# A one-core layer stack on Trainium2: expert gates spread by bf16 one-hot products, the gate in three bf16 parts

## The chip, the cores and the metric

The kernel runs on one core of one Trainium2 chip. The metric is the device time of one execution in microseconds (us). It is computed from fp32 inputs to an fp32 output.

## The reference, cut to what matters

Two blocks follow each other on 512 tokens of width 1024. The first ends in a product-key retrieval of single-neuron experts (`peer_ffn`): each token picks, for each of 8 heads, 16 of 16,384 experts, so 128 experts a token, each with a softmax gate.

```python
def block(args):
    x_blk, i_blk, g_blk = args
    act = jnp.einsum('td,ted->te', x_blk, u[i_blk]).astype(f32)
    hid = jax.nn.gelu(act, approximate=False) * g_blk
    return jnp.einsum('te,ted->td', hid.astype(v.dtype), v[i_blk])
```

An expert's number is 128 times a row index plus a column index, both from 0 to 127.

## The kernel before, in words

All big products are made from operands split into two fp32r halves: `split_hi` (ScalarE, L281) rounds a weight tile of 128x1024 from `wraw` to `wh`, `split_lo` (L289, VectorE or GpSimd) forms the rest `wl`, and `three` (L300 to L302) issues three matmuls, high by high, low by high, high by low. `wh` and `wl` have four buffers, so ScalarE may write the high half of tile m+4 only when TensorE is done with tile m, and VectorE waits for ScalarE.

The experts are computed in two ways. For 384 of the 512 tokens (`ND`), TensorE computes all 16,384 activations x·u as 128 tiles (`up_pe`, L300 to L302 with 384 columns; eight chunks `kc` of three matmuls a tile), ScalarE applies gelu and SyncE stores the result in DRAM. For these tokens the gates must be spread over a matrix of 128x128 per token that is zero but at the 128 chosen experts. The other 128 tokens gather their rows of u by indirect DMA (`fetch_pool`, L1844), and VectorE takes 128 dot products (L1834, 1.22 us each, one or two in a stage, by the table `DOT`).

The gate matrix of a token is one matmul over the 128 slots: the stationary operand holds, for each slot, the one-hot row of its row index times the slot's gate; the moving operand holds the one-hot row of its column index. Both are fp32, and a gate product (`gate_pe`, L1715) shows as two matmul records and two weight loads. The engines walk through the 128 tiles in the same order, each with a list of stages m:

- Slots are turned onto partitions in stages 27, 37 and 47 (`TURN`): TensorE transposes three matrices (row index, column index, gate) of 128 tokens, and ScalarE copies them to `iT` (L1789).
- In 48 of the 73 stages from 48 to 120 (`GATE`: k for stage 48 + 74k/48) VectorE forms the one-hot tiles of eight tokens, group k: two equality comparisons of 128x1024 (L1822), then the product by the gate for tokens 4 to 7 (L1827). ScalarE multiplies tokens 0 to 3 by the gate, one by one (L1780). The tiles have two buffers; one is called `oh`, the other is part of `under`, and VectorE waits until the products of group k-2 are done.
- Two stages later (`GMUL`) TensorE makes the eight gate products of group k, one after each chunk of three matmuls. The first waits for both equalities and the first of ScalarE's products, the fifth for L1827.
- ScalarE copies the banks of four tokens to `gbuf` (L1761), SyncE stores finished blocks of 64 tokens (L1909).

VectorE's order in a stage is: `split_lo` of tile m+4, the second top-k (up to stage 44), the one-hot tiles, the dot products.

```python
    GATE = {48 + k * 74 // NG: k for k in range(NG)}
    GMUL = {m + 2: k for m, k in GATE.items()}
    for _k in range(SP):
        DOT.setdefault(46 + _k * 81 // SP, []).append(_k)
```

Of the 48 groups, 26 come in a stage whose forerunner has none, and 22 in a stage right behind another group's; of these 22, 13 have two dot products in the stage before and 9 have one.

Of the kernel before, what the change touches and what calls it, by code (L numbers as in the profile page):

```python
# [15 lines left out]
SP = 128  # L16
ND = T - SP
# [57 lines left out]
def build_program(nc, A, out):  # L75
    ctx = ExitStack()

    def sb(name, shape, dt=F32, scope=None):
        return (scope or ctx).enter_context(nc.sbuf_tensor(name, shape, dt))

    def sem(name):
        return ctx.enter_context(nc.semaphore(name))
# [17 lines left out]
    under = sb("under", [128, 2, 8, T])  # L100
# [12 lines left out]
    iota = sb("iota", [128, 128])  # L113
# [43 lines left out]
    gsp = sb("gsp", [128, SP], scope=peer)  # L157
    hid = sb("hid", [128, SP], scope=peer)
    turned = ExitStack()
    iT = sb("iT", [128, 3, ND], scope=turned)  # L160
    oha = sb("oh", [128, 2, 8, 128], scope=turned)
    rest = sb("rest", [128, max(4, 3 * NR + 6 * ND - 3 * ND - 2048)], scope=turned)
    top = ExitStack()
    qb = sb("qb", [128, 2, T], scope=top)
# [56 lines left out]
    fetch = [b.rearrange("p a t -> p (a t)") for b in (tmpb[:, 0:2, :], tmpb[:, 2:4, :], rsb[:, 0:2, :], sqdg[:, :, :])]  # L221


    oh = [[oha[:, w, :, :] for w in range(2)], [under[:, w, :, 0:128] for w in range(2)]]

    vg = [vgt[:, i, :] for i in range(4)]
    va = vat[:, 5:7, :].rearrange("p a t -> p (a t)")
# [65 lines left out]
    freed = {}  # L293
# [1288 lines left out]
    s_itp, s_it = sem("s_itp"), sem("s_it")  # L1582
    s_idx, s_gsp = sem("s_idx"), sem("s_gsp")
    s_gl = sem("s_gl")
    s_gas = [sem(f"s_gs{i}") for i in range(NL)]
    s_oh, s_os = sem("s_oh"), sem("s_os")
    s_gm, s_gb, s_gst = sem("s_gm"), sem("s_gb"), sem("s_gst")
    s_rsum, s_rtp, s_rx = sem("s_rsum"), sem("s_rtp"), sem("s_rx")
    s_f = [sem(f"s_f{i}") for i in range(len(fetch))]
# [25 lines left out]
    def second_dve(dve, tc, part):  # L1615

        k2, n0 = tc % 2, SEC_N * tc
        if part == 0:
            if tc == 3:
                dve.wait_ge(s_it, 1)  # L1620
            if tc == 2:
                dve.wait_ge(s_gsp, 16 * (128 // SP))
                dve.wait_ge(s_idx, 2 + 16 * (128 // SP))
            dve.wait_ge(s_top, top_count(15, tc, 5))
            dve.tensor_copy(tif[:, k2, :, :], ti[:, tc, :, :]).then_inc(s_sec, 1)
# [75 lines left out]
    def gate_bank(q):  # L1701
        return 5 + q % 3

    def gate_pe(pe, i):

        k, j = i // 8, i % 8
        b = gate_bank(i // 4)
        if i % 4 == 0:
            bank_free(pe, b)
        if j < 4:  # L1710
            pe.wait_ge(s_oh, 3 * k + 2)
            pe.wait_ge(s_os, 4 * k + j + 1)
        else:
            pe.wait_ge(s_oh, 3 * k + 3)
        pe.matmul(ps[b][:, (i % 4) * 128:(i % 4 + 1) * 128], oh[k % 2][0][:, j, :], oh[k % 2][1][:, j, :], start=True,  # L1715
                  stop=True).then_inc(s_gm, 1)
        freed[b] = (s_gb, i // 4 + 1)

    def up_pe(pe):
        def each(m, kc):  # L1720
            if m == 0 and kc in (1, 5):
                score_pe(pe, 14 if kc == 1 else 15)
            if m in GMUL:
                gate_pe(pe, 8 * GMUL[m] + kc)

        for m in range(128):
            pe_linear(pe, W_U, [m], B_U, None, lambda g: (s_gl, g + 1), t0=SP, each=each)
            if m in TURN:
                tc = TURN[m]
                b = gate_bank(tc)  # L1730
                pe.wait_ge(s_sec, SEC_N * (tc + 1))
                bank_free(pe, b)
                for w in range(3):
                    mm = pe.transpose(ps[b][:, w * 128:(w + 1) * 128], slot[:, tc % 2, w, :], ident[:, :])
                mm.then_inc(s_itp, 1)
                freed[b] = (s_it, tc)
# [15 lines left out]
    def gate_copy(act, q):  # L1752

        half, at = gate_half(4 * q)
        block = 4 * q // BW
        act.wait_ge(s_gm, 4 * q + 4)
        if q == 0:
            act.wait_ge(s_it, 3)
        if block >= 2:
            act.wait_ge(s_gst, 16 * 16 * (block - 1))  # L1760
        act.activation(gb[:, half, :, at:at + 4], ps[gate_bank(q)][:, :].rearrange("p (t i) -> p i t", t=4),  # L1761
                       ACT.Copy).then_inc(s_gb, 1)

    def up_act(act):
        for m in range(128):
            split_hi(act, W_U + m + 4)
            act.wait_ge(s_wuse, W_U + m + 1)
            if m >= NL:
                act.wait_ge(s_gas[m % NL], 16 * (m // NL))
            act.activation(gl[:, m % NL, :], ps[B_U[m]][:, SP:T], ACT.Gelu).then_inc(s_gl, 1)  # L1770
            if m in GMUL:
                gate_copy(act, 2 * GMUL[m])
                gate_copy(act, 2 * GMUL[m] + 1)
            if m in GATE:
                k = GATE[m]
                act.wait_ge(s_oh, 3 * k + 1)
                for j in range(4):
                    t = 8 * k + j
                    o = oh[k % 2][0][:, j, :]
                    act.activation(o, o, ACT.Copy, scale=iT[:, 2, t:t + 1]).then_inc(s_os, 1)  # L1780
            if m in EXPS:
                tc = EXPS[m]
                g = slot[:, tc % 2, 2, :]
                act.wait_ge(s_sec, SEC_N * tc + 50)
                act.activation(g, g, ACT.Exp).then_inc(s_secx, 1)
            if m in TURN:
                tc = TURN[m]
                act.wait_ge(s_itp, tc)
                act.activation(iT[:, :, tc * 128 - SP:tc * 128 + 128 - SP],  # L1789
                               ps[gate_bank(tc)][:, 0:384].rearrange("p (w t) -> p w t", w=3),  # L1790
                               ACT.Copy).then_inc(s_it, 1)
            if m == ROWTURN:
                for half in range(2):
                    act.wait_ge(s_rtp, half + 1)
                    act.activation(xrow[:, half * 512:(half + 1) * 512], ps[6 + half][:, :],
                                   ACT.Copy).then_inc(s_rx, 1)
            if m >= 126:
                hh_act(act, m - 126)

    def up_dve(dve):  # L1800
        for m in range(128):
            if W_U + m + 4 not in U_POOL:
                split_lo(dve, W_U + m + 4)
            if m >= 126:
                h_lo(dve, m - 126)
            if m == ROWSUM:
                x3 = fetch[0].rearrange("p (c t) -> p c t", t=128)
                for c in (14, 15):
                    dve.wait_ge(*XL["q"][c])
                for s in range(128 // SP):  # L1810
                    dve.tensor_tensor(x3[:, :, SP * s:SP * s + SP], Xh[:, :, 0:SP].bitcast(F32),
                                      Xl[:, :, 0:SP].bitcast(F32), ALU.add).then_inc(s_rsum, 1)
            for tc, part in SEC.get(m, ()):
                second_dve(dve, tc, part)
            if m in GATE:
                k = GATE[m]
                if k == 0:
                    dve.wait_ge(s_it, 3)
                if k >= 2:
                    dve.wait_ge(s_gm, 8 * (k - 1))  # L1820
                for w in range(2):
                    dve.tensor_tensor(oh[k % 2][w], iota[:, :].unsqueeze(1).to_broadcast([128, 8, 128]),  # L1822
                                      iT[:, w, 8 * k:8 * k + 8].unsqueeze(2).to_broadcast([128, 8, 128]),
                                      ALU.is_equal).then_inc(s_oh, 1)
                o = oh[k % 2][0][:, 4:8, :]
                dve.wait_ge(s_oh, 3 * k + 1)
                dve.tensor_tensor(o, o, iT[:, 2, 8 * k + 4:8 * k + 8].unsqueeze(2).to_broadcast([128, 4, 128]),  # L1827
                                  ALU.mult).then_inc(s_oh, 1)
            for k in DOT.get(m, ()):
                f = k % len(fetch)  # L1830
                dve.wait_ge(s_f[f], 16 * (k // len(fetch) + 1))
                if k == 0:
                    dve.wait_ge(s_rx, 2)
                dve.tensor_tensor_reduce(out=fetch[f], in0=fetch[f], in1=xrow, scale=1.0, scalar=0.0, op0=ALU.mult,  # L1834
                                         op1=ALU.add, accum_out=hid[:, k:k + 1]).then_inc(s_dot, 1)
            if m >= 125:
# [1111 lines left out]
```

## Time and profile before

| what | value |
|---|---|
| median of 3 runs | 2653.19 us (2648.71 to 2653.51) |
| the profiled execution, first to last instruction (its span) | 2650.9 us |
| TensorE busy | 2604.1 us (98%), 14486 matmul records |
| VectorE busy | 1631.4 us (62%) |
| ScalarE busy | 1075.7 us (41%) |
| GpSimd busy | 1001.7 us (38%) |
| mean granted TensorE clock | 0.995 |

No time of its own other than the span is shown for the profiled execution; the median of the runs is 2.3 us longer than the span. Engines are PE (matmuls), PEld (weight loads), DVE (VectorE), ACT (ScalarE), POOL (GpSimd) and SP (SyncE). A matmul's recorded end is modelled, so starts are the surer reading: the distance from the start of one to the start of the same line's next one tells what a slot of TensorE's work takes.

### The profile page before, as it was taken

The numbers are of one execution on the slowest core, as the hardware profiler recorded it, in microseconds if no ns is written. First come the engines' busy times: TensorE is split into PE (matmuls) and PEld (weight loads), VectorE is DVE, ScalarE is ACT, GpSimd is POOL, SyncE is SP. The second block draws the span as 40 slices with busy tenths as digits, with TensorE's granted clock in tenths as the row PEclk, the third lists the DMA queues.
The fourth block names the chain that finished last, engine by engine and source line by source line (L and its number), as shares of the span: only waits on it lengthen the run. The fifth ranks groups of instructions, "written<-read, shape, count | busy, mean of one in ns | idle before, by whom it ended". The sixth has DMA issues, their size and how long they took to land.

```text
span 2650.9 us, 37746 instructions
## 1 busy us (share of the span) xinstructions
PE 2604.1 (98%) x14486; PEld 2356.1 (89%) x14486; DVE 1631.4 (62%) x2998; ACT 1075.7 (41%) x1758; POOL 1001.7 (38%) x547
## 2 busy tenths in 40 slices
PE   8999999999999999999999999999999999999998
PEld 6779899999999999999999988888889766988887
DVE  6754989898898878888888755710215264630112
ACT  5444334445555543333333443532323355442331
POOL 3323353544444433333333045344442423254442
PEclk9999999999999999999999999999999999999999
DMA  4223355779999989999999433233332321233331
GB/s 149 95 84 90 94 142 158 225 262 314 350 349 349 324 292 336 335 350 347 339 351 346 157 111 95 86 98 96 96 98 76 107 86 49 87 104 95 95 98 53
DMA packets 235473, 488.47 MB, mean 184 GB/s; under 512 B 85128, under 2 KB 135192, under 8 KB 235040
## 3 DMA queue, kind: packets, MB, share of 16 engines
q1 hardware_dynamic: 198432, 351.83, 41.8%
q0 software_dynamic: 36864, 134.23, 13.9%
q8 instruction: 116, 1.90, 0.3%
q14 instruction: 61, 0.50, 0.1%
HBM read 442.98 MB, written 42.88 MB: 183 GB/s over the span
## 4 chain that ended last, share of the span: by engine, by line
PE 93%; DVE 4%; ACT 1%; issue 1%; DMA 0%; POOL 0%; SPq 0%; DVEq 0%; ACTq 0%
PE ps L300 29%; PE ps L302 28%; PE ps L301 28%; PE ps L1715 3%; PE ps L488 1%; PE ps L2554 1%; PE ps L2642 1%; DVE tmpb L1109 1%; PE ps L1528 1%; DVE hT L2287 0%; PE ps L2606 0%; PE ps L534 0%; ACT pt L2622 0%; DVE wl L289 0%; DVE fo L2284 0%
## 5 line engine op out<-in xcount | busy, mean ns | idle before, releaser
L289 POOL TENSOR_TENSOR wl<-wraw,wh 128x1024 fp32r<-128x1024 f32 x254 | 619.7, 2446 | 988.4 <-ACT wh L281 911.6
L281 ACT ACTIVATE wh<-wraw 128x1024 fp32r<-128x1024 f32 x487 | 513.4, 1057 | 1094.1 <-PE ps L302 1071.4
L300 PE MATMUL ps<-Xh,wh 128*128 128x384 f32 (+2 forms) x2336 | 863.3, 370 | 15.4 <-DVE wl L289 9.0
L301 PE MATMUL ps<-Xl,wh 128*128 128x384 f32 (+2 forms) x2336 | 822.0, 352 | 0.0
L302 PE MATMUL ps<-Xh,wl 128*128 128x384 f32 (+2 forms) x2336 | 820.5, 351 | 0.0
L300 PEld LDWEIGHTS ps<-Xh,wh 128*128 128x128 f32 x2336 | 443.3, 190 | 61.0 <-issue 17.4
L302 PEld LDWEIGHTS ps<-Xh,wl 128*128 128x128 f32 x2336 | 442.1, 189 | 39.4
L301 PEld LDWEIGHTS ps<-Xl,wh 128*128 128x128 f32 x2336 | 443.8, 190 | 36.4
L289 DVE TENSOR_TENSOR wl<-wraw,wh 128x1024 fp32r<-128x1024 f32 x233 | 284.8, 1223 | 136.7 <-ACT wh L281 136.1
L300 PE MATMUL ps<-Hh,wh 128*128 128x384 f32 x1024 | 342.8, 335 | 1.6 <-ACT gl L1770 1.6
L302 PE MATMUL ps<-Hh,wl 128*128 128x384 f32 x1024 | 342.1, 334 | 0.0
L301 PE MATMUL ps<-Hl,wh 128*128 128x384 f32 x1024 | 342.1, 334 | 0.0
L2051 POOL DMA_INDIRECT vg<-in_v,idx x128 | 162.4, 1269 | 336.3 <-DVE va L2026 298.4
L2439 DVE SCALAR_TENSOR_TENSOR tmpb<-ps,rsb 128x512 f32<-128x512 f32 x64 | 43.9, 689 | 359.0 <-PE ps L302 359.0
L300 PE MATMUL ps<-Fh,wh 128*128 128x512 f32 (+1 forms) x576 | 210.8, 366 | 0.0
L301 PE MATMUL ps<-Fl,wh 128*128 128x512 f32 (+1 forms) x576 | 210.5, 365 | 0.0
L302 PE MATMUL ps<-Fh,wl 128*128 128x512 f32 (+1 forms) x576 | 210.5, 365 | 0.0
L300 PEld LDWEIGHTS ps<-Hh,wh 128*128 128x128 f32 x1024 | 192.3, 188 | 1.9 <-ACT gl L1770 1.9
L301 PEld LDWEIGHTS ps<-Hl,wh 128*128 128x128 f32 x1024 | 192.3, 188 | 0.0
L302 PEld LDWEIGHTS ps<-Hh,wl 128*128 128x128 f32 x1024 | 192.3, 188 | 0.0
L2026 DVE SCALAR_TENSOR_TENSOR va<-vg,hid,va 128x1024 f32<-128x1024 f32 x127 | 162.3, 1278 | 1.2
L1844 POOL DMA_INDIRECT tmpb<-in_un,idx x64 | 99.4, 1553 | 129.9 <-DVE hid L1834 119.0
(309 smaller groups left out, 3296.8 us busy)
## 6 DMA issues: line engine op xcount, KB each, us to landing
wraw<-in_uT SPq DMA_DIRECT2D x128, 512.0 KB
wraw<-in_v SPq DMA_DIRECT2D x128, 512.0 KB
wraw<-in_up SPq DMA_DIRECT2D x128, 512.0 KB
gA_scratch<-gl SPq DMA_DIRECT2D x122, 192.0 KB
gl<-gA_scratch SPq DMA_DIRECT2D x122, 192.0 KB
gG_scratch<-gbuf SPq DMA_DIRECT2D x64, 256.0 KB
lg<-gG_scratch SPq DMA_DIRECT2D x128, 128.0 KB
wraw<-in_w_q SPq DMA_DIRECT2D x24, 512.0 KB
```

The lines of the kernel that those rows point to most:

```text
L281: act.activation(wh[:, n % 4, :], wraw[:, n % 4, :], ACT.Copy).then_inc(s_wh, 1)
L289: pool.tensor_tensor(wl[:, n % 4, :], wraw[:, n % 4, :], wh[:, n % 4, :].bitcast(F32), ALU.subtract).then_inc(s_wl, 1)
L300: pe.matmul(o, ah, bh, start=start, stop=False)
L301: pe.matmul(o, ah, bl, start=False, stop=False)
L302: return pe.matmul(o, al, bh, start=False, stop=stop)
L488: mm = pe.matmul(ps[b][:, c:c + 1], part[:, cs], ones[:, 0:1], start=p == 0, stop=p == len(parts) - 1)
L1109: dve.scalar_tensor_tensor(out=acc[:, k:T], in0=buf[:, 0:T - k], scalar=col("cw", 6 * (3 - k) + CONV[i]), in1=acc[:, k:T], op0=ALU.mult, o ...
L1715: pe.matmul(ps[b][:, (i % 4) * 128:(i % 4 + 1) * 128], oh[k % 2][0][:, j, :], oh[k % 2][1][:, j, :], start=True, stop=True).then_inc(s_gm, 1)
L1844: pool.indirect_dma_start(out=fetch[k % nf], out_offset=None, in_=A["un"], in_offset=bass.IndirectOffsetOnAxis(ap=idx[:, k:k + 1], axis=0) ...
L2026: dve.scalar_tensor_tensor(out=va, in0=vg[k % 4], scalar=hid[:, k:k + 1], in1=va, op0=ALU.mult, op1=ALU.add).then_inc(s_va, 1)
L2051: pool.indirect_dma_start(out=vg[k % 4], out_offset=None, in_=A["v"], in_offset=bass.IndirectOffsetOnAxis(ap=idx[:, k:k + 1], axis=0)).the ...
L2439: dve.scalar_tensor_tensor(out=tmpb[:, k % 4, :], in0=ps[bu[m]][:, :], scalar=0.0, in1=RS, op0=ALU.max, op1=ALU.mult).then_inc(s_fe[layer], 1)
```

## The change

The gate is split into three bf16 parts whose sum is the fp32 gate. ScalarE's copies at a turn become three: the gate in fp32 (`gr`), its bf16 rounding (`gT[:, 0]`) and the two index matrices in bf16 (`iT`). In the stage behind a turn VectorE forms the second and third part (`parts_dve`, three small operations, and once a doubled `iota` in bf16). The one-hot tiles are bf16, with pairs of tokens innermost. VectorE forms all of them for a group: equality for the column index (`hot[3]`), equality for the row index (`hot[0]`), then `hot[3]` times each part of the gate, the third in place. ScalarE's four products go away. A token takes three bf16 matmuls with the same stationary tile, summed in PSUM, and the first token of a group waits for all five VectorE operations.

```diff
-    iT = sb("iT", [128, 3, ND], scope=turned)
-    oha = sb("oh", [128, 2, 8, 128], scope=turned)
+    iT = sb("iT", [128, 2, ND], BF16, scope=turned)
+    gT = sb("gT", [128, 3, ND], BF16, scope=turned)
+    gr = sb("gr", [128, 128], scope=turned)
+    iotaX = sb("iotaX", [128, 128, 2], BF16, scope=turned)
+    oha = sb("oh", [128, 4, 4, 128, 2], BF16, scope=turned)
...
-        if j < 4:
-            pe.wait_ge(s_oh, 3 * k + 2)
-            pe.wait_ge(s_os, 4 * k + j + 1)
-        else:
-            pe.wait_ge(s_oh, 3 * k + 3)
-        pe.matmul(ps[b][:, (i % 4) * 128:(i % 4 + 1) * 128], oh[k % 2][0][:, j, :], oh[k % 2][1][:, j, :], start=True,
-                  stop=True).then_inc(s_gm, 1)
+        if j == 0:
+            pe.wait_ge(s_oh, 5 * k + 5)
+        for w in range(3):
+            mm = pe.matmul(ps[b][:, (i % 4) * 128:(i % 4 + 1) * 128], oh[k % 2][0][:, j // 2, :, j % 2],
+                           oh[k % 2][1 + w][:, j // 2, :, j % 2], start=w == 0, stop=w == 2)
+        mm.then_inc(s_gm, 1)
...
-            if m in GATE:
-                k = GATE[m]
-                act.wait_ge(s_oh, 3 * k + 1)
-                for j in range(4):
-                    t = 8 * k + j
-                    o = oh[k % 2][0][:, j, :]
-                    act.activation(o, o, ACT.Copy, scale=iT[:, 2, t:t + 1]).then_inc(s_os, 1)
...
-                act.activation(iT[:, :, tc * 128 - SP:tc * 128 + 128 - SP],
-                               ps[gate_bank(tc)][:, 0:384].rearrange("p (w t) -> p w t", w=3),
+                ts = slice(tc * 128 - SP, tc * 128 + 128 - SP)
+                if tc > 1:
+                    act.wait_ge(s_part, 3 * (tc - 1))
+                act.activation(gr[:, :], ps[gate_bank(tc)][:, 256:384], ACT.Copy).then_inc(s_it, 1)
+                act.activation(gT[:, 0, ts], ps[gate_bank(tc)][:, 256:384], ACT.Copy).then_inc(s_it, 1)
+                act.activation(iT[:, :, ts], ps[gate_bank(tc)][:, 0:256].rearrange("p (w t) -> p w t", w=2),
                                ACT.Copy).then_inc(s_it, 1)
...
+            if m - 1 in TURN:
+                parts_dve(dve, TURN[m - 1])
             if m in GATE:
...
-                for w in range(2):
-                    dve.tensor_tensor(oh[k % 2][w], iota[:, :].unsqueeze(1).to_broadcast([128, 8, 128]),
-                                      iT[:, w, 8 * k:8 * k + 8].unsqueeze(2).to_broadcast([128, 8, 128]),
+                hot = oh[k % 2]
+                for o, w in ((hot[3], 1), (hot[0], 0)):
+                    dve.tensor_tensor(o, iotaX[:, :, :].unsqueeze(1).to_broadcast([128, 4, 128, 2]), of_slot(iT[:, w, :]),
                                       ALU.is_equal).then_inc(s_oh, 1)
-                o = oh[k % 2][0][:, 4:8, :]
-                dve.wait_ge(s_oh, 3 * k + 1)
-                dve.tensor_tensor(o, o, iT[:, 2, 8 * k + 4:8 * k + 8].unsqueeze(2).to_broadcast([128, 4, 128]),
-                                  ALU.mult).then_inc(s_oh, 1)
+                dve.wait_ge(s_oh, 5 * k + 1)
+                for w in (0, 1):
+                    dve.tensor_tensor(hot[1 + w], hot[3], of_slot(gT[:, w, :]), ALU.mult).then_inc(s_oh, 1)
+                dve.wait_ge(s_oh, 5 * k + 4)
+                dve.tensor_tensor(hot[3], hot[3], of_slot(gT[:, 2, :]), ALU.mult).then_inc(s_oh, 1)
...
+    def parts_dve(dve, tc):
+
+        n, ts = 3 * (tc - 1), slice(tc * 128 - SP, tc * 128 + 128 - SP)
+        if tc == 1:
+            dve.tensor_copy(iotaX[:, :, :], iota[:, :].unsqueeze(2).to_broadcast([128, 128, 2])).then_inc(s_iob, 1)
+        dve.wait_ge(s_it, 3 * tc)
+        dve.tensor_tensor(gr[:, :], gr[:, :], gT[:, 0, ts], ALU.subtract).then_inc(s_part, 1)
+        dve.wait_ge(s_part, n + 1)
+        dve.tensor_copy(gT[:, 1, ts], gr[:, :]).then_inc(s_part, 1)
+        dve.wait_ge(s_part, n + 2)
+        dve.tensor_tensor(gT[:, 2, ts], gr[:, :], gT[:, 1, ts], ALU.subtract).then_inc(s_part, 1)
```

`of_slot(row)` reads the eight tokens of the group as four pairs, each pair repeated 128 times with the pair innermost.

## Rows read from the trace of the kernel before

**Rows 1.** The page's parts 1 and 4: busy times; the chain that ended last, by line.

```profile
PE 2604.1 (98%) x14486; PEld 2356.1 (89%) x14486; DVE 1631.4 (62%) x2998; ACT 1075.7 (41%) x1758; POOL 1001.7 (38%) x547
...
PE ps L300 29%; PE ps L302 28%; PE ps L301 28%; PE ps L1715 3%; PE ps L488 1%; PE ps L2554 1%; PE ps L2642 1%; DVE tmpb L1109 1%; PE ps L1528 1%; DVE hT L2287 0%; PE ps L2606 0%; PE ps L534 0%; ACT pt L2622 0%; DVE wl L289 0%; DVE fo L2284 0%
```

**Rows 2.** The chain of 551 to 952 us, by line.

```profile
by line: PE ps L300 26.0%; PE ps L301 25.8%; PE ps L302 25.4%; PE ps L1715 22.5%; issue 0.3%
```

**Rows 3.** Stretch 700 to 800: us; PE, PEld, DVE, ACT, POOL busy; clock, DMA share, GB/s.

```profile
700.00:800.00 100.00, 99.75 (x637) 98.05 (x636) 87.90 (x113) 51.99 (x107) 46.82 (x30) 1.00 1.07 344
```

**Rows 4.** Waits of 551 to 952 us: who waited for whom, us, times, longest.

```profile
ACT wh L281 <- PE ps L302: 93.2, 35, 4.2
DVE wl L289 <- ACT wh L281: 44.5, 26, 2.4
PEld ps L1715 <- issue: 5.2, 14, 0.4
```

**Rows 5.** One forming of gate tiles, 706.8 to 712 us, in order of time.

```profile
706.85 1.06 ACT L281 ACTIVATE wh<-wraw 128x1024 fp32r<-128x1024 f32 x1 [3.56 <-PE ps L302]
...
707.95 1.22 DVE L289 TENSOR_TENSOR wl<-wraw,wh 128x1024 fp32r<-128x1024 f32 x1 [2.40 <-ACT wh L281]
...
709.09 2.35 DVE L1822 TENSOR_TENSOR under<-iota,iT 128x1024 f32<-128x1024 f32 x2
...
711.19 0.19 PEld L302 LDWEIGHTS ps<-Xh,wl 128*128 128x128 f32 x1
...
711.36 0.68 DVE L1827 TENSOR_TENSOR under<-under,iT 128x512 f32<-128x512 f32 x1
...
711.51 0.30 PEld L1715 LDWEIGHTS ps<-under 128*128 128x128 f32 x2
```

**Rows 6.** The next forming, 715 to 718 us, in order of time.

```profile
715.39 2.35 DVE L1822 TENSOR_TENSOR oh<-iota,iT 128x1024 f32<-128x1024 f32 x2
...
717.26 0.19 PEld L302 LDWEIGHTS ps<-Xh,wl 128*128 128x128 f32 x1
...
717.81 0.30 PEld L1715 LDWEIGHTS ps<-oh 128*128 128x128 f32 x2 [0.36 <-issue]
```

**Rows 7.** The instructions on the one-hot tiles (both tiles called oh): ns min/median/max.

```profile
L1715 PE MATMUL ps<-oh x384: 270/273/348, 553.6 to 940.7; 128*128 128x128 f32 x192
L1822 DVE TENSOR_TENSOR oh<-iota,iT x48: 1215/1217/1219, 551.2 to 933.2; 128x1024 f32<-128x1024 f32 x48
L1827 DVE TENSOR_TENSOR oh<-oh,iT x24: 679/683/685, 553.5 to 934.3; 128x512 f32<-128x512 f32 x24
L1661 DVE TENSOR_TENSOR oh<-baf,iob x8: 2282/2283/2284, 399.6 to 529.4; 128x2048 bf16<-128x2048 bf16 x8
L1668 DVE TENSOR_TENSOR oh<-oh,tif x8: 1224/1224/1225, 401.9 to 531.7; 128x2048 bf16<-128x2048 bf16 x8
```

**Rows 8.** TensorE's matmuls with a gate product per slot, and without one.

```profile
701.20 0.33 PE L302 MATMUL ps<-Xh,wl 128*128 128x384 f32 x1
...
701.37 0.38 PE L1715 MATMUL ps<-oh 128*128 128x128 f32 x2
...
701.94 0.33 PE L302 MATMUL ps<-Xh,wl 128*128 128x384 f32 x1
...
707.17 0.33 PE L302 MATMUL ps<-Xh,wl 128*128 128x384 f32 x1
...
707.69 0.35 PE L302 MATMUL ps<-Xh,wl 128*128 128x384 f32 x1
```

**Rows 9.** Weight loads around products of one column, and products of 256 columns.

```profile
1650.96 0.31 PEld L488 LDWEIGHTS ps<-ones,sqdg 128*128 128x128 f32 x2
...
1652.31 0.19 PEld L300 LDWEIGHTS ps<-Xh,wh 128*128 128x128 f32 x1
...
1650.84 0.28 PE L301 MATMUL ps<-Xl,wh 128*128 128x256 f32 x1
1650.96 0.28 PE L302 MATMUL ps<-Xh,wl 128*128 128x256 f32 x1
```

More of the change, by code:

```diff
@@ L221, in build_program @@
     fetch = [b.rearrange("p a t -> p (a t)") for b in (tmpb[:, 0:2, :], tmpb[:, 2:4, :], rsb[:, 0:2, :], sqdg[:, :, :])]
-    oh = [[oha[:, w, :, :] for w in range(2)], [under[:, w, :, 0:128] for w in range(2)]]
+    oh = [[oha[:, w, :, :, :] for w in range(4)],
+          [under[:, w // 2, 4 * (w % 2):4 * (w % 2) + 4, 0:128].bitcast(BF16).rearrange("p c (i t) -> p c i t", t=2)
+           for w in range(4)]]
     vg = [vgt[:, i, :] for i in range(4)]
@@ L1585, in build_program @@
     s_gas = [sem(f"s_gs{i}") for i in range(NL)]
-    s_oh, s_os = sem("s_oh"), sem("s_os")
+    s_oh, s_part = sem("s_oh"), sem("s_part")
     s_gm, s_gb, s_gst = sem("s_gm"), sem("s_gb"), sem("s_gst")
@@ L1619, in second_dve @@
             if tc == 3:
-                dve.wait_ge(s_it, 1)
+                dve.wait_ge(s_it, 3)
             if tc == 2:
@@ L1735, in up_pe @@
                 mm.then_inc(s_itp, 1)
-                freed[b] = (s_it, tc)
+                freed[b] = (s_it, 3 * tc)
             if m == ROWTURN:
@@ L1757, in gate_copy @@
         if q == 0:
-            act.wait_ge(s_it, 3)
+            act.wait_ge(s_it, 9)
         if block >= 2:
@@ L1817, in up_dve, with of_slot @@
                 if k == 0:
-                    dve.wait_ge(s_it, 3)
+                    dve.wait_ge(s_it, 9)
+                    dve.wait_ge(s_part, 9)
+                    dve.wait_ge(s_iob, 2)
                 if k >= 2:
                     dve.wait_ge(s_gm, 8 * (k - 1))
-                for w in range(2):
-                    dve.tensor_tensor(oh[k % 2][w], iota[:, :].unsqueeze(1).to_broadcast([128, 8, 128]),
-                                      iT[:, w, 8 * k:8 * k + 8].unsqueeze(2).to_broadcast([128, 8, 128]),
-                                      ALU.is_equal).then_inc(s_oh, 1)
-                o = oh[k % 2][0][:, 4:8, :]
-                dve.wait_ge(s_oh, 3 * k + 1)
-                dve.tensor_tensor(o, o, iT[:, 2, 8 * k + 4:8 * k + 8].unsqueeze(2).to_broadcast([128, 4, 128]),
-                                  ALU.mult).then_inc(s_oh, 1)
+                def of_slot(row):
+                    return row[:, 8 * k:8 * k + 8].rearrange("p (c t) -> p c t", t=2).unsqueeze(2).to_broadcast(
+                        [128, 4, 128, 2])
+                hot = oh[k % 2]
+                for o, w in ((hot[3], 1), (hot[0], 0)):
+                    dve.tensor_tensor(o, iotaX[:, :, :].unsqueeze(1).to_broadcast([128, 4, 128, 2]), of_slot(iT[:, w, :]),
+                                      ALU.is_equal).then_inc(s_oh, 1)
+                dve.wait_ge(s_oh, 5 * k + 1)
[3 more added lines that the diff above has]
+                dve.tensor_tensor(hot[3], hot[3], of_slot(gT[:, 2, :]), ALU.mult).then_inc(s_oh, 1)
             for k in DOT.get(m, ()):
```

## The prediction

> **What bounds the kernel now.** I read the page's busy times and the chain of the whole program first: TensorE is busy 98%, and the chain is its three lines of the split product, with the gate product L1715 at 3% [rows 1]. The reader is to see that nothing off TensorE has a share that matters. Then I cut the chain to the stretch that the change touches, 551 to 952 us: L1715 is 22.5% of it, and only 0.3% is no work of TensorE [rows 2]. In a window inside it TensorE is busy 99.75 of 100 us at granted clock 1.00, which is 2.4 GHz, and VectorE 87.90 [rows 3]. So TensorE is the bound, but VectorE is a close second, and the waits decide what happens when its work moves [rows 4]: ScalarE waits 35 times for TensorE to give a weight buffer back, VectorE 26 times for ScalarE's high half, and TensorE 14 times, 5.2 us in all, on a gate product.
>
> The 26 are the groups whose forerunner stage has none. For one of these the timeline shows a closed chain [rows 5]: tile m ends, ScalarE, idle for 3.56 us until then, splits the high half at 706.85, VectorE, idle for 2.40 us, forms the low half at 707.95, the two equalities follow at 709.09 and end at 709.09 + 2.35 = 711.44, and the gate's weight load starts at 711.51, 0.07 later. The load of L302 before it began at 711.19, and loads follow each other at about 0.17, so the natural start was 711.37. TensorE already waits 0.14 us here, for the second equality. In the group behind, the equalities start 6.30 us later (715.39), end at 717.74, and the load starts at 717.81, again 0.07 later, 0.36 after its natural moment [rows 6]. This is the case of the 13 groups with two dot products between; together with the first group they are the 14 waits. The other 9 have slack.
>
> **The change, part by part.**
>
> *When a group's tiles are ready.* Now the first product needs two equalities: 2.35 us from the start of the first. After, it needs five operations of 1024 bf16 elements. The price: an fp32 operation of 1024 elements takes 1.217 us, of 512 elements 0.683; one of 2048 bf16 elements with packed innermost runs takes 1.224 (the product L1668), as long as 1024 of fp32, but the equality L1661, one of whose operands repeats an element innermost, takes 2.283 [rows 7]. The new tiles put pairs innermost for all operands, so I take the faster rate for all five: 0.683 us each. The far bound is 1.217 each, the near bound four elements at once, which no row shows: 1.217 - 0.683 is 0.534 for 512 steps, so 256 steps less is 0.267 less, 0.42. Operations that don't wait start 0.08 before the end of the one before (711.36 to 711.96 is 0.60 for a 0.683 one, by the dot product that follows; the same shows in 2.35 = 1.14 + 1.217 [rows 5]). The fifth works in place and waits for the fourth's end, 0.03 more. Ready after 3 x 0.60 + 0.683 + 0.03 + 0.683 = 3.20 us, against 2.35: 0.85 later. The chain ahead of it (ScalarE, low half) is not shortened by anything: both engines were idle before their step. So each of the 26 groups costs TensorE 0.85 more: **22.1 us**.
>
> *VectorE's own load.* It is held 3.12 us for a group instead of 2.27 + 0.60 = 2.87, 0.25 more. In the 13 groups with two dot products between, the next tiles come 6.55 us after the last instead of 6.30, and TensorE's own pace stays under that: 13 x 0.25 = **3.3 us**. The 9 with one dot product (1.15 us less, 5.40) stay under TensorE's pace of 6.30 - 0.36 = 5.94. If the spare time were gone, the cost would be 48 x 0.25 = 12 us.
>
> *TensorE's slot.* A slot of three split products takes 0.52 us (707.17 to 707.69), one with a gate product 0.74 (701.20 to 701.94), say 0.225 for the gate [rows 8]; 384 of these are 86 us. After, it is three bf16 products, each with its own load: the page counts as many loads as matmuls, 14486 [rows 1], though L300 and L301 use the same stationary operand, so the repeat in the new products saves no load. The stream: 256 columns take 0.120 a product, 384 columns 0.173, so 128 columns are 0.053 and 0.013 is fixed: 0.066. The load: 12 loads of fp32 weights around one-column products go from 1650.96 to 1652.31, 0.112 each, and the fp32r load behind them is not quicker [rows 9]. Two-byte weights are not in this trace. Bounds: 0.112 each, that is no gain, so 3 x 0.112 = 0.336 a token; or wholly hidden, 3 x 0.066 = 0.198. My value takes a load as its bytes, half of 0.112, an estimate; it then hides under a stream of 0.066, but the fp32r load behind the third product has only that stream as cover and still takes 0.112: 2 x 0.066 + 0.112 = 0.244, 0.019 more than now, 0.15 a tile of eight. It counts for 26 + 9 = 35 tiles, since in the 13 others it disappears in the longer wait: **5.3 us**. I put this value above the slow bound because every other price of that row is one of four-byte data.
>
> In this trace short products run at the pace of their loads. The Trainium skill (TensorE: Matmul & The Clock Gate, Back-to-back issue gap) has a rule that speaks against the change: a stream of load and product pairs of 128 columns keeps about 81 ns a pair, more than the columns take. No row here shows such a pair in bf16. By it the slot would be 2 x 0.081 + 0.112 = 0.274, and the sum 8 us higher.
>
> *ScalarE.* Four products a group go, and the waits before them; nobody on the path waits for them now but the first product, whose wait ends on VectorE anyway. Worth nothing: what covers it is ScalarE's 3.56 us of idle time ahead of the split. Its three copies at a turn, in place of one, lie a whole tile ahead of the first group.
>
> *The parts.* In stage 48 three operations of 128 elements stand before group 0: 0.683 - 384 x 0.00104 (the slope of the two fp32 rows) is 0.28 each, **0.85 us** on the path of the first group, whose tiles are now formed from 551.2 on. In stages 28 and 38 they and the copy of `iota` are behind a TensorE that is never short of work there; if that cover were gone, 2 us. SyncE's and GpSimd's lists keep their order; GpSimd's gathers wait for dot products, which come up to 0.25 us later and have VectorE's order as their only reader. No DMA is added.
>
> **The sum:** 22.1 + 3.3 + 5.3 + 0.85 = 31.6 us. The durations are from one execution with a span of 2650.9 us; the runs' median is 2.3 above that, and I add to the median: 2653.2 + 31.6 = 2684.8, **2685 us**.
>
> **The rivals.**
>
> 1. *Slow bf16 loads.* If a load of 128 two-byte weights takes 0.112 us as the fp32 ones do, a token costs 0.336, 0.111 more than now, 0.89 a tile. 35 tiles give 31.1 us, the 13 waiting ones 0.89 less the 0.61 that they wait, 3.6. With 26.3 of VectorE's terms: 61 us, 2714. For it: the only load price in the trace. Against: only four-byte rows. The Trainium skill (same page, Weight-path perf modes) says that 128 weights of a type other than fp32 load in a faster way, with any column step up to 1,024; this lowers the rival's chance, and no run here shows it yet. Chance 0.25.
>
> 2. *The equalities stay at one element a step,* as L1661 did: 0.54 more for two of the five. Then 39 groups are 1.08 later, 42 us more, and the 9 lose their slack (5.40 + 1.08 against 6.09, 0.39 each, 3.5 us): 31.6 + 45.6, 2730. If all five do, the tiles are 2.68 later than forecast, 39 x 2.68 + 9 x 1.99 = 122 us more: 2807. For: L1661 is the trace's only bf16 equality. Against: its operand repeats singly, the new one in pairs. Chance 0.10.
>
> 3. *Faster.* VectorE takes bf16 at four elements a step, 0.42 us. Then the tiles are ready after 3 x 0.34 + 0.42 + 0.03 + 0.42 = 1.89 us, under the 2.35 - 0.14 at which TensorE stops waiting; the waits of now, 26 x 0.14 and 13 x 0.36, go (-8.3 us). With loads wholly hidden, 0.198 a token, another 48 x 8 x 0.027 = -10.4: 2634. It decides at a ready time of 2.35. No row shows such a rate for two tensor operands: 0.05. The quick slot alone, with VectorE as forecast, gives 26.3 - 7.6 = +19 us, 2672; it is inside the range.
>
> 4. *Nothing to be measured:* the wait for all five is covered because TensorE reaches the group later than I read. Rows 5 and 6 speak against it: 0.03.
>
> **The numbers.** 0.57 for my forecast (2672 to 2693, with the 0.198 and 0.274 slots inside), 0.25, 0.10, 0.05, 0.03. The range takes the first two with the slow case's own spread of some 6 us: 2668 to 2720. About 0.2% (5 us) is what a measurement of this kernel can tell from no change; slower by more has 0.92, faster 0.05, within 0.03.
>
> **What would show it.** In the profile after: five operations a group near 0.68 us; the first weight load of a group 0.07 us behind the end of the fifth in some 39 groups; idle time before L1715's loads of about 26 x 0.99 + 13 x 0.6, 33 us where 5.2 stand now; slots with a gate product of 0.52 + 0.24 us; no L1780, ScalarE's idle longer; VectorE busy longer by under 20 us. Wrong if bf16 loads follow each other at 0.11, if an equality takes 1.2 us, or if TensorE doesn't wait.

## The result and the profile after

The changed kernel takes 2680.09 us (median of 4 runs, 2678.67 to 2683.81), the kernel before 2652.03 in the same comparison: a ratio of 1.0111, with a 95% interval of 1.0099 to 1.0124. It is 28 us slower.

The page of the changed kernel: its span, the busy times, and the chain that ended last by engine and by line. The three split products are now L305 to L307, the gate product is L1718.

```profile
span 2678.7 us, 38245 instructions
...
PE 2606.7 (97%) x14870; PEld 2301.3 (86%) x14870; DVE 1644.6 (61%) x3104; ACT 1019.4 (38%) x1572; POOL 996.9 (37%) x547
...
PE 85%; DVE 11%; ACT 2%; issue 1%; DMA 0%; POOL 0%; SPq 0%; ACTq 0%; DVEq 0%
PE ps L305 27%; PE ps L306 26%; PE ps L307 26%; DVE wl L294 2%; PE ps L1718 2%; ACT wh L286 1%; DVE oh L1837 1%; DVE oh L1833 1%; DVE under L1837 1%; DVE under L1833 1%; PE ps L493 1%; PE ps L2577 1%; PE ps L2665 1%; DVE tmpb L1114 1%; DVE tmpb L1845 1%
```

TensorE's recorded busy share is 97% against 98%, yet its part of the chain is only 85%, and VectorE's one-hot tiles (L1833, L1837) and the split ahead of them (L286, L294) stand in the chain. The same line of the kernel before:

```profile
PE 93%; DVE 4%; ACT 1%; issue 1%; DMA 0%; POOL 0%; SPq 0%; DVEq 0%; ACTq 0%
```

The answer to [rows 4], the waits from 551 to 980 us (who waited for whom, us, times, longest):

```profile
ACT wh L286 <- PE ps L307: 274.7, 73, 6.5
...
PEld ps L1718 <- issue: 91.1, 384, 2.3
...
PE ps L1718 <- DVE oh L1839: 14.1, 21, 2.0
PE ps L1718 <- DVE under L1839: 11.4, 18, 1.1
```

Where the loads of the gate product waited 5.2 us, the view now has 91.1. Not all of it is a wait for tiles: 0.16 us stand before the first load of each of the 384 slots, some 60 us (the slot below shows one). The starts give the wait itself. Summed over the groups, the first load comes 30.7 us later than in a slot inside a tile. 39 products (21 and 18) wait for L1839, the fifth VectorE operation. That is 26 + 13 groups. One group of the 26, answering to [rows 5] in order of time:

```profile
700.80 1.06 ACT L286 ACTIVATE wh<-wraw 128x1024 fp32r<-128x1024 f32 x1 [4.14 <-PE ps L307]
...
701.89 1.23 DVE L294 TENSOR_TENSOR wl<-wraw,wh 128x1024 fp32r<-128x1024 f32 x1 [2.24 <-ACT wh L286]
...
703.04 1.28 DVE L1833 TENSOR_TENSOR under<-iotaX,iT 128x1024 bf16<-128x1024 bf16 x2
...
704.24 1.29 DVE L1837 TENSOR_TENSOR under<-under,gT 128x1024 bf16<-128x1024 bf16 x2
...
705.12 0.19 PEld L307 LDWEIGHTS ps<-Xh,wl 128*128 128x128 f32 x1
...
705.56 0.69 DVE L1839 TENSOR_TENSOR under<-under,gT 128x1024 bf16<-128x1024 bf16 x1
...
706.37 0.18 PEld L1718 LDWEIGHTS ps<-under 128*128 128x128 bf16 x3 [1.06 <-issue]
```

Tile m ends, ScalarE splits at 700.80, VectorE forms the low half at 701.89 and begins the tiles at 703.04. The fifth operation ends at 705.56 + 0.69 = 706.25, and the first gate load starts at 706.37. From the start of the forming to that load it is 3.33 us, where [rows 5] have 2.42. The gap to the load before, at 705.12, is 1.25 us, where a slot inside the tile has 0.35.

The instructions on the one-hot tiles, answering to [rows 7] (ns min/median/max, first and last start):

```profile
L1718 PE MATMUL ps<-oh x576: 217/220/234, 554.7 to 968.9; 128*128 128x128 bf16 x192
L1833 DVE TENSOR_TENSOR oh<-iotaX,iT x48: 680/683/693, 551.4 to 960.1; 128x1024 bf16<-128x1024 bf16 x48
L1837 DVE TENSOR_TENSOR oh<-oh,gT x48: 680/683/686, 552.6 to 961.3; 128x1024 bf16<-128x1024 bf16 x48
L1839 DVE TENSOR_TENSOR oh<-oh,gT x24: 691/692/695, 553.9 to 962.0; 128x1024 bf16<-128x1024 bf16 x24
```

All bf16 operations of 1024 elements run in 0.683 to 0.692 us at the median, the equalities too. A slot with a gate product, answering to [rows 8], by its loads:

```profile
709.10 0.19 PEld L307 LDWEIGHTS ps<-Xh,wl 128*128 128x128 f32 x1
709.45 0.17 PEld L1718 LDWEIGHTS ps<-under 128*128 128x128 bf16 x3 [0.16 <-issue]
709.58 0.19 PEld L305 LDWEIGHTS ps<-Xh,wh 128*128 128x128 f32 x1
709.69 0.19 PEld L306 LDWEIGHTS ps<-Xl,wh 128*128 128x128 f32 x1
709.87 0.19 PEld L307 LDWEIGHTS ps<-Xh,wl 128*128 128x128 f32 x1
```

From one load of L307 to the next it is 0.77 us, 0.247 more than the 0.52 of a slot without a gate (the median of all such slots is 0.760, so 0.240 more). The load of L1718 starts 0.35 behind that of L307, where otherwise the load behind L307 (L302 before) follows at 0.17. Three of them take 0.13 to 0.14, and L306's load follows L305's at 0.11.

**Where the 28 us are.** I took the start of each group's first gate load in both traces and compared the distances from one group to the next. The 25 groups behind a stage without a group (the first of the 26 apart) come 22.8 us later in all, 0.91 each; the 13 with two dot products between 3.4 us, 0.26 each; the 9 others 1.8 us, 0.20 each; the first group is 1.1 us late. At the last group that is 29.1 us, and at the end of the span 27.8. ScalarE's busy time fell from 1075.7 to 1019.4 us, and in these distances nothing became shorter.

### The profile page after: what moved, and what is told of

Its sections match the earlier page's. It is cut to its first block, busy times and chain, and to the rows that moved or that the text cites. A ratio compares the mean times of both kernels' runs of the same rounds, so it can differ in the third digit from the quotient of the medians.

```text
span 2678.7 us, 38245 instructions
## 1 busy us (share of the span) xinstructions
PE 2606.7 (97%) x14870; PEld 2301.3 (86%) x14870; DVE 1644.6 (61%) x3104; ACT 1019.4 (38%) x1572; POOL 996.9 (37%) x547
## 4 chain that ended last, share of the span: by engine, by line
PE 85%; DVE 11%; ACT 2%; issue 1%; DMA 0%; POOL 0%; SPq 0%; ACTq 0%; DVEq 0%
PE ps L305 27%; PE ps L306 26%; PE ps L307 26%; DVE wl L294 2%; PE ps L1718 2%; ACT wh L286 1%; DVE oh L1837 1%; DVE oh L1833 1%; DVE under L1837 1%; DVE under L1833 1%; PE ps L493 1%; PE ps L2577 1%; PE ps L2665 1%; DVE tmpb L1114 1%; DVE tmpb L1845 1%
## 5 line engine op out<-in xcount | busy, mean ns | idle before, releaser
L286 ACT ACTIVATE wh<-wraw 128x1024 fp32r<-128x1024 f32 x487 | 514.0, 1059 | 1280.0 <-PE ps L307 1278.3
L294 POOL TENSOR_TENSOR wl<-wraw,wh 128x1024 fp32r<-128x1024 f32 x254 | 619.8, 2446 | 983.1 <-ACT wh L286 906.5
L305 PE MATMUL ps<-Xh,wh 128*128 128x384 f32 (+2 forms) x2336 | 861.6, 369 | 16.0 <-DVE wl L294 9.4
L306 PE MATMUL ps<-Xl,wh 128*128 128x384 f32 (+2 forms) x2336 | 820.8, 351 | 0.0
L307 PE MATMUL ps<-Xh,wl 128*128 128x384 f32 (+2 forms) x2336 | 820.1, 351 | 0.0
L305 PEld LDWEIGHTS ps<-Xh,wh 128*128 128x128 f32 x2336 | 441.9, 189 | 62.4 <-issue 18.0
L307 PEld LDWEIGHTS ps<-Xh,wl 128*128 128x128 f32 x2336 | 441.6, 189 | 38.9
L306 PEld LDWEIGHTS ps<-Xl,wh 128*128 128x128 f32 x2336 | 443.6, 190 | 36.4
L294 DVE TENSOR_TENSOR wl<-wraw,wh 128x1024 fp32r<-128x1024 f32 x233 | 284.8, 1223 | 153.6 <-ACT wh L286 153.4
L305 PE MATMUL ps<-Hh,wh 128*128 128x384 f32 x1024 | 342.8, 335 | 1.6 <-ACT gl L1774 1.6
L307 PE MATMUL ps<-Hh,wl 128*128 128x384 f32 x1024 | 342.1, 334 | 0.0
L306 PE MATMUL ps<-Hl,wh 128*128 128x384 f32 x1024 | 342.1, 334 | 0.0
L305 PE MATMUL ps<-Fh,wh 128*128 128x512 f32 (+1 forms) x576 | 210.8, 366 | 0.0
L306 PE MATMUL ps<-Fl,wh 128*128 128x512 f32 (+1 forms) x576 | 210.5, 365 | 0.0
L307 PE MATMUL ps<-Fh,wl 128*128 128x512 f32 (+1 forms) x576 | 210.5, 365 | 0.0
L305 PEld LDWEIGHTS ps<-Hh,wh 128*128 128x128 f32 x1024 | 192.3, 188 | 1.9 <-ACT gl L1774 1.9
L306 PEld LDWEIGHTS ps<-Hl,wh 128*128 128x128 f32 x1024 | 192.3, 188 | 0.0
L307 PEld LDWEIGHTS ps<-Hh,wl 128*128 128x128 f32 x1024 | 192.3, 188 | 0.0
```

The lines of the kernel that those rows point to most:

```text
L286: act.activation(wh[:, n % 4, :], wraw[:, n % 4, :], ACT.Copy).then_inc(s_wh, 1)
L294: pool.tensor_tensor(wl[:, n % 4, :], wraw[:, n % 4, :], wh[:, n % 4, :].bitcast(F32), ALU.subtract).then_inc(s_wl, 1)
L305: pe.matmul(o, ah, bh, start=start, stop=False)
L306: pe.matmul(o, ah, bl, start=False, stop=False)
L307: return pe.matmul(o, al, bh, start=False, stop=stop)
```

## The experiments

Theory 1 says that the time goes into one wait: the first product of a group needs all five VectorE operations, which end 0.92 us later than the two equalities did. The rival, theory 2, says that the three bf16 products with their loads are what costs.

### Undoing the wait by distance: `a_lead3` and `b_lead3`

```diff
-    GMUL = {m + 2: k for m, k in GATE.items()}
+    GMUL = {m + 3: k for m, k in GATE.items()}
...
-            STORE[_last + 3 + _i] = (_b, _i)
+            STORE[_last + 4 + _i] = (_b, _i)
...
-            if m == 123:
+            if m == 124:
                 for j in range(3):
```

The changed kernel with this edit:

> The changed kernel, its gate products made three stages after the tiles are formed instead of two. Theory 1 (the cost is that the first product of a group waits for all five VectorE operations, 0.92 us later than it waited for two): the waits go, 25 x 0.90, 13 x 0.44 and 2.1 for the first group, 30 us off 2680, so 2650. Theory 2 (the three bf16 products and their loads cost the time): the products are the same, so 2670 or more.

Measured: 2651.59 us, ratio 1.0001 (0.9991 to 1.0011). The whole loss is gone with the wait (no first load of a group is late any more); every product and every VectorE operation is still there. Theory 2 falls as the main cause.

The kernel before with the same edit:

> The kernel before with the same three stages. It waits 26 x 0.15 and 13 x 0.38 us, 9 in all, which go: 2643. With no waits on either side, the distance to the changed kernel with three stages is the slot alone: 384 x (0.765 - 0.747) = 7 us by the starts in the two traces. Theory 2 would have some 25.

Measured: 2648.68 us, ratio 0.9989 (0.998 to 0.9999). The distance of the two is 3 us, under the 7 expected, and the kernel before gained less than its 9 us. The waits of `a_lead3` from 551 to 960 us show what took the rest:

```profile
ACT wh L286 <- DMA wraw<-in_uT: 49.2, 12, 7.5
...
PEld ps L1718 <- ACT gbuf L1765: 5.1, 4, 2.4
```

ScalarE, whose split waited for TensorE alone before, now waits 12 times for the transfer of a weight tile, 49.2 us. Its copies of the gate banks stand behind those splits, and TensorE waits for a copy. In `b_lead3` it is 12 times and 30.3 us. In the kernel before no such wait stands in [rows 4]: with the stretch shorter than in the changed kernel, transfers have begun to set the pace in places.

### The wait alone, put into the kernel before: `b_waitall`

```diff
-        if j < 4:
-            pe.wait_ge(s_oh, 3 * k + 2)
-            pe.wait_ge(s_os, 4 * k + j + 1)
-        else:
+        if j == 0:
             pe.wait_ge(s_oh, 3 * k + 3)
+            pe.wait_ge(s_os, 4 * k + 4)
```

> The kernel before, with one part of the change alone: the first gate product of a group waits for everything that VectorE and ScalarE form. Theory 1: first loads come 0.07 us after L1827's end instead of the second equality's, 0.60 later in 26 groups, 15.6 us: 2668. Theory 2: 2652, since no product changes.

Measured: 2666.3 us, ratio 1.0052 (1.0035 to 1.0068). Its waits from 551 to 975 us have this line, where [rows 4] have 14 waits and 5.2 us:

```profile
PEld ps L1713 <- issue: 24.4, 39, 1.0
```

In the 39 groups the first load comes 0.07 us behind the end of VectorE's product, 0.49 behind the end of ScalarE's fourth, so it is VectorE that ends the wait. Summed over the groups, the first gate load comes 24.9 us after its earliest moment (0.175 behind the load before) instead of 9.2: 15.7 more, as worked out. In fp32, with not one product or VectorE operation changed, waiting for the whole group costs half of what the change costs; the change's tiles take 0.3 us longer still.

### Ready earlier, VectorE held longer: `a_halves`

VectorE forms tokens 0 to 3 with five operations of 512 elements, then 4 to 7 with five more, and TensorE waits for each half by itself.

```diff
-        if j == 0:
-            pe.wait_ge(s_oh, 5 * k + 5)
+        if j % 4 == 0:
+            pe.wait_ge(s_oh, 10 * k + 5 + 5 * (j // 4))
...
+                for h in range(2):
+                    n = 10 * k + 5 * h
+                    hot = [o[:, 2 * h:2 * h + 2, :, :] for o in oh[k % 2]]
...
```

> The changed kernel, VectorE forming tokens 0 to 3 with five operations of 512 elements, then 4 to 7 with five more. The first half is ready after about 1.9 us instead of 3.2, but VectorE is held some 3.5 us instead of 3.1. Theory 1: the waits of the 25 go (22 us), the 13 keep theirs: 2658. If VectorE's total work were the cause, it would be slower than 2680 (48 x 0.4 = 19 us more).

Measured: 2656.72 us, ratio 1.0021 (1.0011 to 1.0031). Its instructions on the `oh` tile (equalities and products):

```profile
L1836 DVE TENSOR_TENSOR oh<-iotaX,iT x96: 416/419/426, 550.0 to 938.9; 128x512 bf16<-128x512 bf16 x96
L1839 DVE TENSOR_TENSOR oh<-oh,gT x96: 415/418/422, 550.7 to 939.5; 128x512 bf16<-128x512 bf16 x96
```

Ten operations of 0.42 us hold VectorE longer than five of 0.68, and the kernel is 23 us faster than the changed one. So the cost is not VectorE's total, but when the first product's tiles are ready. The 13 groups and the first keep a wait: 14 late first loads are left, and they add up to 7.5 us.

### Forming ahead of the low half: `a_first` and `b_first`

The block under `if m in GATE` (and the gate's parts) moves ahead of `split_lo` in VectorE's stage; nothing else changes.

```diff
         for m in range(128):
+            if m - 1 in TURN:
+                parts_dve(dve, TURN[m - 1])
+            if m in GATE:
+                k = GATE[m]
...
             if W_U + m + 4 not in U_POOL:
                 split_lo(dve, W_U + m + 4)
```

> The changed kernel, VectorE forming a group's tiles (and the gate's parts) ahead of the stage's low half instead of behind it. The forming then no longer stands behind the chain of tile end, ScalarE's high half and VectorE's low half. Theory 1: all waits go as with three stages, 2650. Theory 2: 2670 or more.

Measured: 2649.05 us, ratio 0.999 (0.998 to 0.9999). VectorE's order in this run:

```profile
701.76 1.29 DVE L1820 TENSOR_TENSOR under<-iotaX,iT 128x1024 bf16<-128x1024 bf16 x2
702.96 1.29 DVE L1824 TENSOR_TENSOR under<-under,gT 128x1024 bf16<-128x1024 bf16 x2
704.29 0.69 DVE L1826 TENSOR_TENSOR under<-under,gT 128x1024 bf16<-128x1024 bf16 x1
705.55 1.23 DVE L294 TENSOR_TENSOR wl<-wraw,wh 128x1024 fp32r<-128x1024 f32 x1 [0.58 <-ACT wh L286]
```

The tiles are formed from 701.76 to 704.98, and only then does VectorE wait for ScalarE's high half (0.58 us ahead of 705.55). No first load waits for tiles any more; the stretch from the first gate load to the last takes 395.3 us, against 425.4 with the change and 397.3 before.

> The kernel before with its tiles formed ahead of the low half. Its waits go (9 us by the starts), unless the weight loads now set the pace: in the runs with three stages ScalarE came to wait for the transfer of a weight tile up to 12 times. 2643 to 2648. The changed kernel in the same order took 2649; the distance is the slot, 384 x 0.018 = 7 us, less what the transfers take back.

Measured: 2645.42 us, ratio 0.998 (0.9971 to 0.9989), against 2649.82 for the kernel before in that comparison. No group's first load is late, but the fifth product of one group comes 4.4 us behind the load before it: TensorE waits for a copy of a gate bank (L1761), and there are four waits of ScalarE for a weight transfer. The two ratios, 0.999 and 0.998, are too near each other to price the slot.

### The products together: `a_end` and `b_end`

```diff
-            if m in GMUL:
-                gate_pe(pe, 8 * GMUL[m] + kc)
+            if m in GMUL and kc == 7:
+                for j in range(8):
+                    gate_pe(pe, 8 * GMUL[m] + j)
```

> The changed kernel, all eight tokens' products behind the tile's last chunk instead of one token behind each chunk. The waits go (the first product comes 3.6 us later in its tile). In the trace the first bf16 load of a slot starts 0.345 us after the load of L307 instead of 0.173, so it is not taken ahead of the fp32r product; here that happens once a tile instead of eight times. If this switch is the price, 24 products take about 24 x 0.058 + 0.2 = 1.6 us instead of 8 x 0.245 = 1.96, and the time is 2633. If each product costs 0.082 wherever it stands, 2650.

Measured: 2641.78 us, ratio 0.996 (0.9945 to 0.9975). The result lies between the two expectations. The weight loads around one group's 24 products:

```profile
700.09 0.19 PEld L307 LDWEIGHTS ps<-Xh,wl 128*128 128x128 f32 x1
700.43 1.39 PEld L1718 LDWEIGHTS ps<-oh 128*128 128x128 bf16 x24 [0.16 <-issue]
701.78 0.19 PEld L305 LDWEIGHTS ps<-Xh,wh 128*128 128x128 f32 x1
701.89 0.19 PEld L306 LDWEIGHTS ps<-Xl,wh 128*128 128x128 f32 x1
```

The late start (0.34 from 700.09 to 700.43) comes once. Then 24 loads take 1.35 us, 0.056 each. In all, a group costs 701.89 - 700.09 = 1.80 us less the 0.35 of two plain steps, 1.45, or 0.18 a token instead of 0.247. Apart, a token pays 0.17 for its late first load, 0.13 for three loads, and gets 0.06 back because the load behind L305's follows at 0.11 instead of 0.17. Together, the 0.17 is paid once a group, the 0.06 comes once as well, and a load keeps 0.056 instead of 0.045: 7 x (0.17 - 0.06 - 0.034) is the 0.53 by which 1.45 lies below 8 x 0.247.

> The kernel before with its products behind the last chunk. The fp32 gate loads are taken ahead in its trace, so nothing is saved on the switch: eight products at 0.225, waits gone, 2643. If the switch costs fp32 as well, less.

Measured: 2643.85 us, ratio 0.9972 (0.996 to 0.9985), as expected, and the same view:

```profile
704.47 0.19 PEld L302 LDWEIGHTS ps<-Xh,wl 128*128 128x128 f32 x1
704.64 1.92 PEld L1715 LDWEIGHTS ps<-oh 128*128 128x128 f32 x16
706.49 0.19 PEld L300 LDWEIGHTS ps<-Xh,wh 128*128 128x128 f32 x1
706.60 0.19 PEld L301 LDWEIGHTS ps<-Xl,wh 128*128 128x128 f32 x1
```

The first load is on time (704.64), and 16 take 1.85 us, 0.116 each: a group costs 706.60 - 704.47 = 2.13 less 0.35, 1.78, what it cost apart (8 x 0.225). Nothing is saved by standing together. Between the two runs the products should make 48 x 0.33 = 16 us, and 2 us came out. In `a_end` the waits from 551 to 960 us have these:

```profile
ACT wh L286 <- DMA wraw<-in_uT: 83.4, 21, 7.4
...
PEld ps L1718 <- issue: 15.0, 48, 4.7
...
PE ps L1718 <- DVE oh L1840: 6.7, 2, 4.4
```

Summed over the 48 groups, `a_end` takes 12 us more than 48 x 1.80, and `b_end` 3 us more than 48 x 2.13. The largest loss is one first load that waits 4.7 us for VectorE and starts at 755.36: ScalarE had waited 5.85 us for a weight tile, and VectorE then 4.91 us for ScalarE. Behind this wait TensorE's granted clock is 0.50, that is 1.2 GHz, from 756 to 759 us, and the fp32r loads follow each other at 0.32 us instead of 0.17. So the expectation of 2633 failed in the main for what lies beside the products: ScalarE, and with it the chain behind it, waits for weight transfers. These losses explain 9 of the 14 us; from the first gate load to the last it is 383.5 us against 389.9, and the rest, outside the gate stretch in the main, is not explained.

### One product instead of three: `a_one`

```diff
-        for w in range(3):
+        for w in range(1):
...
-                           oh[k % 2][1 + w][:, j // 2, :, j % 2], start=w == 0, stop=w == 2)
+                           oh[k % 2][1 + w][:, j // 2, :, j % 2], start=True, stop=True)
```

> The changed kernel with only the first of the three products of a token; the second and third part of the gate are formed but left out of the result. It prices a bf16 product where it stands: two products less of 0.060 each a token, 0.96 us a tile, which counts in the 25 and 9 tiles that aren't followed by a wait, 33 us: 2647. The first load's wait stays near 1.25 us in the 25 groups. If the price of a token were the switch between types and not the products, only a few us go.

Measured: 2656.36 us, ratio 1.0016 (1.0007 to 1.0026). The loads of one slot:

```profile
701.92 0.19 PEld L307 LDWEIGHTS ps<-Xh,wl 128*128 128x128 f32 x1
702.26 0.10 PEld L1718 LDWEIGHTS ps<-oh 128*128 128x128 bf16 x1 [0.15 <-issue]
702.26 0.20 PEld L305 LDWEIGHTS ps<-Xh,wh 128*128 128x128 f32 x1
702.56 0.19 PEld L307 LDWEIGHTS ps<-Xh,wl 128*128 128x128 f32 x1
```

From load to load of L307 it is 0.64 us here. At the median a slot takes 0.65, in the changed kernel 0.76, so two products less are 0.055 each. I expected 33 us off, at 0.060 a product, and 24 came. All 48 groups now start late. Summed over the groups, the first load comes 48.2 us after its earliest moment (0.345 behind the load before), in the changed kernel 30.7: a shorter tile only waits longer, and those of the 9 groups wait too.

### Stride or type: `a_contig`

```diff
+            lo = 64 * (j % 2)
-            mm = pe.matmul(..., oh[k % 2][0][:, j // 2, :, j % 2],
-                           oh[k % 2][1 + w][:, j // 2, :, j % 2], start=w == 0, stop=w == 2)
+            mm = pe.matmul(..., oh[k % 2][0][:, j // 2, lo:lo + 64, :].rearrange("p i t -> p (i t)"),
+                           oh[k % 2][1 + w][:, j // 2, lo:lo + 64, :].rearrange("p i t -> p (i t)"), start=w == 0, stop=w == 2)
```

> The changed kernel with both operands of the gate products read as 128 elements in a row instead of every second one, so the products are of other elements and the gates are wrong in the result; all counts and sizes stay. Theory 3a (the first bf16 load starts 0.345 us behind the one of L307 because the types change): nothing moves, 0.345 and 0.057, 2680. Theory 3b (the stride of two is what holds the load or slows it): 0.173, and a slot shorter by some 0.06 to 0.17 us, which takes 34 tiles x 8 x 0.06 = 16 us or more off.

Measured: 2682.68 us (two runs), ratio 1.0122 (1.0105 to 1.014).

```profile
698.44 0.19 PEld L307 LDWEIGHTS ps<-Xh,wl 128*128 128x128 f32 x1
698.79 0.17 PEld L1719 LDWEIGHTS ps<-oh 128*128 128x128 bf16 x3 [0.16 <-issue]
698.92 0.19 PEld L305 LDWEIGHTS ps<-Xh,wh 128*128 128x128 f32 x1
```

The load of the gate product starts 0.35 behind that of L307 as before, and three take 0.13. The stride of two costs nothing. That the change of type holds the first load back is what is left of the two theories; no run had bf16 products between other bf16 products of 384 columns, so it stays an inference from `a_end` and this run. That a bf16 load is never taken ahead of an fp32r product, whatever stands before, would look the same.

### Both moves: `a_endfirst`

> The changed kernel with both moves: tiles formed ahead of the low half, and the eight tokens' products behind the last chunk. The products behind the last chunk gave 2641.8, with one wait for VectorE of 4.4 us and ScalarE waiting 83 us for weight transfers; the earlier forming takes that one wait away: 2636 to 2641. If the transfers set the pace now, no faster than 2641.

Its edits are those of `a_end` and `a_first` together. Measured: 2642.53 us, ratio 0.9969 (0.9958 to 0.9979). Its waits from 551 to 960 us:

```profile
ACT wh L286 <- DMA wraw<-in_uT: 106.3, 28, 8.1
...
PEld ps L1718 <- ACT gbuf L1766: 13.1, 6, 4.0
```

The earlier forming adds nothing. ScalarE waits 28 times for a weight tile's transfer, and TensorE loses 13.1 us inside its gate products behind gate copies that stand behind those splits. From here the transfers of this stretch seem to be what to work on: in `a_end` the DMA share of 545 to 960 us is 1.01, at 337 GB/s, where 0.98 and 328 stood before. But no run changed them, and a transfer is also issued only when VectorE's low half has freed its buffer (SyncE waits 50 times for that in `a_end`, 163.8 us), so which of the two makes a tile late is not shown.

`a_end` is 11 us faster than the kernel before, `a_endfirst` 7, and `b_end`, which has nothing of the change but the same order of products, 9. The three intervals overlap: no run here shows the bf16 gate faster than the fp32 gate in the same order.

## Why the prediction was right, point by point

The forecast was 2685 us, 31.6 more than before; it came out at 2680, 28 more, by the mechanism that was forecast.

- **Ready 0.85 us later, 22.1 us.** Measured 0.91 to 0.92 a group and 22.8 us. The five operations cost 0.683 as taken, the fifth ends 3.22 us after the first begins (forecast 3.20), and TensorE starts 0.12 behind it where 0.07 was taken. The first loads wait 30.7 us in all, where the prediction had 33. `b_waitall`, `a_lead3`, `a_first` and `a_halves` show that it is this wait.
- **VectorE's longer hold, 3.3 us.** 0.26 for each of 13 groups, 3.4 us.
- **TensorE's slot, 5.3 us.** The price of a gate product was near, 0.240 to 0.247 against 0.244, but by luck. The prediction took 0.066 as the least that a product needs and 0.112 for the fp32r load behind; the loads pace at 0.056 in `a_end`, and the first of a slot is late by 0.17, which I did not have. The Trainium skill (TensorE: Matmul & The Clock Gate, Back-to-back issue gap) gives about 81 ns for a pair of load and product of 128 columns. That does not show here: the pairs of `a_end` keep 0.056 us, and the measurement decides. The Trainium skill's faster load of 128 weights that are not fp32 (same page, Weight-path perf modes) is in accord with the traces: 0.056 a pair in `a_end`, 0.116 for fp32 in `b_end`.
- **The step that failed** is "It counts for 26 + 9 = 35 tiles". In the 9 it is 0.20 each, 1.8 us. In the 25 it is nothing: their 0.91 is the later readiness alone (3.33 less 2.42). From the first gate load of such a tile to the fp32r load behind its last it is 5.47 us, against 5.45 before (medians). The first slot of a waiting tile is cheaper in bf16. From its gate load to the next fp32r load it is 0.14 in the group above, where the kernel before has 711.51 [rows 5] to this load:

```profile
711.73 0.19 PEld L300 LDWEIGHTS ps<-Xh,wh 128*128 128x128 f32 x1
```

  0.22. The medians are 0.15 and 0.22, and the 0.07 between them pays back most of the 7 x 0.013 that the tile's other slots cost more (0.760 against 0.747). This term was mis-sized by 3.5 us; the sum was 3.6 us too high.
- **The parts, 0.85 us.** In the stage of the first group, by the timeline:

```profile
550.39 0.28 DVE L1856 TENSOR_TENSOR gr<-gr,gT 128x128 f32<-128x128 f32 x1
550.71 0.23 DVE L1858 CAST gT<-gr 128x128 bf16<-128x128 f32 x1
550.97 0.29 DVE L1860 TENSOR_TENSOR gT<-gr,gT 128x128 bf16<-128x128 f32 x1
551.35 1.29 DVE L1833 TENSOR_TENSOR oh<-iotaX,iT 128x1024 bf16<-128x1024 bf16 x2
```

  From 550.39 to 551.35 it is 0.96 us. The first group comes only 1.1 us late with this and its own forming (0.92), since VectorE came to this stage 0.8 us earlier in this execution.
- **ScalarE's relief** was taken as worth nothing, and the groups' distances have no gain in them. No run tests it alone.
- **The rivals.** Slow bf16 loads: 0.056 to 0.058, not 0.112. Equalities at half rate: 0.683 us, not 1.217. Four elements a step: no. Covered waits: 39 groups wait.

## What to carry to other kernels

Where a stream engine makes the operands of a bound engine, look up in the trace which operation the first use waits for; adding work there is paid in full even when the stream engine is busy for only 62% of the time, and moving the first use or the forming by one place in the order takes it all back. Keep bf16 products together instead of one behind each chunk of fp32r ones; for fp32 products it saved nothing. After such a wait is gone, look at once for the next one: here it was the wait for weight tiles.

## What the runs showed of the hardware

- Weight loads of 128 bf16 columns with products of 128 columns follow each other at 0.056 us (24 in a row, `a_end`), fp32 ones at 0.116 (16 in a row, `b_end`). Three bf16 ones behind an fp32r product take 0.13 us with a stride of two elements and without one (`a_contig`).
- The first bf16 load behind an fp32r product of 384 columns starts 0.345 us after that product's own load, where an fp32 or fp32r load starts at 0.173 to 0.178. I had not expected it, and its cause is open. A step behind the gate product is 0.06 us shorter than elsewhere, behind fp32 ones too. By the groups of `a_end`, a bf16 token that stands apart costs 0.06 to 0.07 us more than one in a row (0.240 to 0.247 against 0.18).
- A VectorE operation of two bf16 tensors whose innermost run is a pair, in one operand repeated 128 times, runs 1024 elements in 0.683 us, an equality as well as a product; the equality L1666 with a singly repeated operand still takes 2.284 for 2048.
- After TensorE had waited 4.7 us in `a_end`, its granted clock was 0.50 from 756 to 759 us; in the changed kernel, whose waits last 2.3 us at most, it is 1.00 from 545 to 960 us.
